# Element order of the expert-gate product in a one-core PEER block: tokens innermost instead of blocks

## The reference, cut to what matters

```
act = jax.nn.gelu(jnp.einsum('td,thkd->thk', xc, u[e]))
return jnp.einsum('thk,thkd->td', g * act, v[e])
```

## Time and profile before

| | us |
|---|---|
| median of 3 runs | 1191.55 |
| lowest and highest run | 1191.1, 1193.72 |
| span of the profiled execution (first to last instruction) | 1189.5 |
| PE busy (share of the span) | 1116.6 (94%) |
| DVE busy | 958.8 (81%) |
| ACT busy | 659.2 (55%) |
| POOL busy | 362.5 (30%) |

### The profile page before, as it was taken

One profiled execution on the slowest core, in us unless ns is written; L12 is line 12 of the kernel. 1 busy time (PEld: TensorE's weight loads), 2 busy tenths in 40 slices (PEclk: granted clock), 3 DMA queues, 4 the chain that ended last, 5 costly groups with the idle time before them and its releaser, 6 DMA issues.

```text
span 1189.5 us, 21986 instructions
## 1 busy us (share of the span) xinstructions
PE 1116.6 (94%) x7174; PEld 982.8 (83%) x7174; DVE 958.8 (81%) x1701; ACT 659.2 (55%) x1042; POOL 362.5 (30%) x324
## 2 busy tenths in 40 slices
PE   6999999989999999999999999788888888999998
PEld 6687887879999999999999999566666666888887
DVE  5645666666899989899999999999999999444444
ACT  4255665664344444566666666666655665554443
POOL 0000122000001116523333333544444443555553
PEclk9999999999999999999999999999999999999999
DMA  7563222454445555544444444333333335555553
GB/s 258 171 202 124 72 71 92 140 177 154 166 147 172 190 182 183 186 142 142 143 154 144 141 152 149 106 125 123 123 126 130 130 125 171 187 195 192 193 193 123
DMA packets 50016, 181.34 MB, mean 152 GB/s; under 512 B 5552, under 2 KB 5680, under 8 KB 49968
## 3 DMA queue, kind: packets, MB, share of 16 engines
q1 hardware_dynamic: 49968, 180.72, 45.5%
HBM read 178.60 MB, written 2.10 MB: 152 GB/s over the span
## 4 chain that ended last, share of the span: by engine, by line
PE 49%; issue 24%; DVE 23%; ACT 1%; DVEq 1%; DMA 1%; POOL 0%; SPq 0%; ACTq 0%
PE bank L679 15%; DVE gsum L1428 7%; DVE big L1436 5%; DVE lo L1298 4%; PE bank L628 4%; PE bank L322 4%; PE bank L629 3%; PE bank L630 3%; PE bank L324 3%; PE bank L323 3%; PE bank L571 1%; DVE same L1410 1%; DVE oneA L1419 1%; DMA raw<-wpre_d 1%; PE bank L336 1%
## 5 line engine op out<-in xcount | busy, mean ns | idle before, releaser
L925 ACT ACTIVATE hi<-raw 128x1024 fp32r<-128x1024 f32 x253 | 267.9, 1060 | 353.4 <-PE bank L679 185.3
L1298 DVE TENSOR_TENSOR lo<-raw,hi 128x1024 fp32r<-128x1024 f32 x253 | 315.5, 1252 | 104.9 <-ACT hi L925 104.1
L628 PE MATMUL bank<-xhi,hi 128*128 128x256 f32 x1024 | 293.9, 287 | 0.8 <-DVE lo L1298 0.8
L629 PE MATMUL bank<-xlo,hi 128*128 128x256 f32 x1024 | 289.5, 283 | 0.0
L630 PE MATMUL bank<-xhi,lo 128*128 128x256 f32 x1024 | 289.3, 282 | 0.0
L1543 POOL TENSOR_TENSOR auxl<-big,auxh 128x256 fp32r<-128x256 f32 x128 | 139.8, 1093 | 222.2 <-ACT auxh L947 222.1
L1528 POOL TENSOR_TENSOR oneB<-kep,eT 128x512 fp32r<-128x512 f32 x128 | 154.0, 1204 | 167.0 <-PE bank L642 157.5
L628 PEld LDWEIGHTS bank<-xhi,hi 128*128 128x128 f32 x1024 | 196.1, 191 | 2.2 <-issue 1.2
L629 PEld LDWEIGHTS bank<-xlo,hi 128*128 128x128 f32 x1024 | 196.2, 192 | 0.0
L630 PEld LDWEIGHTS bank<-xhi,lo 128*128 128x128 f32 x1024 | 196.0, 191 | 0.0
L679 PE MATMUL bank<-hi,auxh 128*128 128x512 f32 x508 | 161.2, 399 | 3.9 <-ACT hi L925 3.4
(11 more groups left out here) (234 smaller groups left out, 1744.8 us busy)
## 6 DMA issues: line engine op xcount, KB each, us to landing
raw<-u_d SPq DMA_DIRECT2D x128, 512.0 KB, 3.3
raw<-v_d SPq DMA_DIRECT2D x128, 512.0 KB, 3.3
raw<-wpre_d SPq DMA_DIRECT2D x78, 512.0 KB, 3.7
big<-x_d SPq DMA_DIRECT2D x2, 512.0 KB, 3.9
out_d<-big SPq DMA_DIRECT2D x2, 512.0 KB, 5.1
big<-out_d SPq DMA_DIRECT2D x2, 512.0 KB, 5.1
out_d<-big SPq DMA_DIRECT2D x4, 256.0 KB, 2.1
big<-cst_d SPq DMA_DIRECT2D x1, 719.5 KB, 6.9
```

The source lines that it names most:

```text
L628: pe.matmul(out, wh, xhi[:, k, :], start=(k == 0), stop=False)
L629: pe.matmul(out, wh, xlo[:, k, :], start=False, stop=False)
L925: act.activation(hi[:, n % SPLIT, :], raw[:, n % RING, :], ACT.Copy).then_inc(hi_done, 1)
L1298: dve.tensor_tensor(lo[:, n % SPLIT, :], raw[:, n % RING, :], hi[:, n % SPLIT, :].bitcast(F32), ALU.subtract).then_inc(lo_done, 1)
```

## The change

`weigh` reads and writes the same 256 elements of `big`, but walks them with the block outside and the four tokens inside; before, the token was outside and the 64 blocks inside. `gsum` is laid out in the new order, and so `add_parts` reads the PSUM bank in that order (block, token, part, in place of token, block, part). Nothing else is edited: the same instructions, operand sizes, waits and increments.

```diff
-        gsum = sb("gsum", [P, 4, HALF])
+        gsum = sb("gsum", [P, HALF, 4])
...
-            by_token = big[:, :].rearrange("p (e t) -> p t e", t=T)
+            by_block = big[:, :].rearrange("p (e t) -> p e t", t=T)
...
-                parts = bank[6 + g % 2][:, :].rearrange("p (t r e) -> p t e r", t=4, r=2)
+                parts = bank[6 + g % 2][:, :].rearrange("p (t r e) -> p e t r", t=4, r=2)
                 dve.tensor_reduce(gsum[:, :, :], parts, AXX, ALU.add).then_inc(S("bank67_read"), 1)
...
-                w4 = by_token[:, bass.ds(i * (4 * UNROLL) + 4 * (g % NGRP), 4), e0:e0 + HALF]
+                w4 = by_block[:, e0:e0 + HALF, bass.ds(i * (4 * UNROLL) + 4 * (g % NGRP), 4)]
                 dve.tensor_tensor(w4, gsum[:, :, :], w4, ALU.mult).then_inc(S("weighed"), 1)
```

## The result

The median went from 1191.72 us (4 runs, 1191.1 to 1193.72) to 1161.64 us (4 runs, 1160.83 to 1162.21): a ratio of 0.9745, 95% interval 0.9731 to 0.9759. The forecast was 1160 in a range of 1146 to 1178. The profiled execution of the kernel after has a span of 1159.0 us, 30.5 less than before.

The account below looks back on a forecast made before the run. VectorE was taken to bound the u+g and v+g stages, TensorE the last. Gains of 15.9 + 14.4 + 1.5 = 31.8 us take the span from 1189.5 to 1157.7, median 1160 us, range 1146 to 1178.

Parts of the forecast that it names:

- The product's own time: VectorE's product beside an idle GpSimd: falls from 0.75 us to 0.42 us, that of adjacent elements.
- the reduce: VectorE's 512 reads out of PSUM in the new order: stays at 0.67 to 0.68 us.
- Its cause: The product's extra 0.33 to 0.34 us comes with walking big in strides of 1024 bytes, 1.3 ns an element.
- the half-gain rival: Only reads or only writes recover: product 0.59 us, gain 18 us, time 1174; chance 0.07.
- The u+g stage: Step falls from 3.587 to 3.33 us, TensorE then bounds; 62 steps give 15.9 us.
- The v+g stage: Step falls from 4.168 to 3.92 us; 58 steps give 14.4 us, 9 to 18 by the bounds.
- The chain: v+g stage: row build, gate matmuls, hi, auxh, auxl, compare, oneB, product's rest; two steps take 7.85 us.
- The joints: Two products into the v+g stage and three at its end, each 0.3 us shorter, partly hidden: 1.5 us.
- first rival: v+g product slowed by contention, not fully waiting: falls to some 0.42 us, gain 57 us, time 1135; chance 0.07.
- the rests of 0.51 and 0.21 us: Product's time left after the GpSimd instruction ahead of it ends: 0.51 us before, 0.21 us forecast after.
- the turn: Rival, v+g stage: auxl comes after the compare, step 4.44 us, 16 us lost there, about 1190; chance 0.04.
- The reduce pays nothing for jumps of 512 bytes: Rival, both middle stages: reduce pays for new jumps, 0.68 us longer, loss of 44 us, 1235; chance 0.07.

Follow-up runs that it names:

- e3: Kernel before, with the product writing into gsum instead of big, so only the reads of big jump: 1181.02 us.
- e4: Kernel before, with both inputs of the product taken from gsum, so only the writes to big jump: 1169.74 us.
- e1: Kernel after, with gsum's layout and the reduce put back as before, so only the walk over big is new: 1172.83 us.
- e7: Kernel after, with 16 in place of 24 matmuls per u tile in the u+g stage: 1156.42 us.
- e9: Kernel after, with ScalarE's copy to auxh put ahead of its hi in each v+g step: 1156.40 us.
- e5: Kernel after, with GpSimd's distances in the v+g stage cut from 512 to 4 elements: 1133.10 us.
- e6: Kernel before, with GpSimd's distances in the v+g stage cut from 512 to 4 elements: 1160.09 us.
- e11: Kernel after, with the v+g stage's distances made by ScalarE instead of GpSimd and auxh put ahead of hi: 1131.44 us.
- e12: Kernel before, with the v+g stage's distances made by ScalarE instead of GpSimd and auxh put ahead of hi: 1145.12 us.

## Why the prediction was right

- *The product's own time* was taken as 0.42 and is 0.412; the reduce as unchanged and is 678 ns. Right.
- *Its cause* was put down to the walk over `big`, at 1.3 ns an element. e3 and e4 show that this is a sum of two prices, 0.20 us for the reads and 0.12 for the writes; e1 shows that the reads of `gsum` would have paid as well, had its layout not been turned along. The forecast didn't price that layout; with the old one (e1) the time is 1172.83, near the 1174 of the half-gain rival, though for another reason.
- *The u+g stage.* 3.33 forecast, 3.312 measured, 62 x 0.275 = 17.1 us in place of 15.9. That TensorE takes over is seen in the gate matmuls without a wait, and in e7.
- *The v+g stage.* 3.92 forecast, 3.958 measured: 12.2 us in place of 14.4. The chain is the right one (e9), and mis-sized by 0.08 in two steps: `hi` 0.03 later, `auxl` 0.02 longer, the compare 0.03 later behind it.
- *The joints.* What is left of the 30.5 us, 30.5 - 17.1 - 12.2 = 1.2 us, against 1.5 forecast. The sum comes out as near as it does, 30.5 for 31.8, in part because the errors of the two stages, 1.2 too little and 2.2 too much, have opposite signs.
- *The rivals.* The product still stands still, 1.26 us (first rival out): e5 and e6 show that it is `oneB` that holds it, the rests of 0.51 and 0.21 us that it waits and then works. `auxl` stays ahead of `oneB` and starts before the compare, so the turn hasn't slipped. The reduce pays nothing for jumps of 512 bytes.

## What to carry to other kernels

In these runs a VectorE product that walks an SBUF tile element by element in strides of 256 or 1024 bytes pays for each jumping stream by itself; turn the loops until at least two, better four, float32 are adjacent, in every operand, the scratch tile too. An instruction that looks long may be mostly a stand behind GpSimd: compare it with the same instruction beside an idle GpSimd before pricing it. What a faster instruction is worth is decided by what else fills the step: the same 0.33 us gave 0.275 a step in the u+g stage, where TensorE took over, 0.21 in the v+g stage, where a chain did, and nothing in the v+g stage of e11 against that of e12.

## What the runs showed that was not expected

Jumping writes are cheaper than they look: in e4 the product's record is 0.61 us long, but the next instruction starts 0.45 after it began; in the kernel after the two are 0.41 and 0.33. VectorE's records overlap the next one by 0.08 to 0.16 us, so prices are better read from starts. And taking GpSimd's long instruction away (e5) moves the wait instead of ending it: the compare then stands behind `auxl`. A wait that the profile books as issue, as in e11, can have a releaser all the same: look at what ended just before on the other engines.
